# Two tiles of a second block: products of the identity with zeros in front of TensorE's sums and weight waits

## The reference, cut to what matters

```
for l in range(DEPTH):                                   # DEPTH = 2
    ...                                                  # attention, retention, y
    h_res = h_res + y
    hf = rms_norm_2(h_res, ffn_norm_g[l])
    gate, up = jnp.split(hf @ w_gate_up[l], 2, axis=-1)  # 1024 x 5632
    h_res = h_res + (jax.nn.silu(gate) * up) @ w_down[l] # 2816 x 1024
return h_res[:, N_META:]
```

## Time and profile before

| | us |
|---|---|
| median of 3 runs | 2458.93 |
| the profiled execution | 2453.13 |
| its span | 2451.3 |
| TensorE matmul busy | 2145.9 (88%) |
| VectorE busy | 1576.1 (64%) |
| mean granted TensorE clock | 0.947 of full speed |

### The profile page before, as it was taken

How to read it: one execution, slowest core, us unless ns; L and a number is a source line. 1 busy time by engine, 2 the same in 40 slices (tenths; PEclk the granted TensorE clock), 3 DMA queues, 4 the chain that set the end, 5 groups by cost and what they waited for, 6 DMA issues and landing times. The chain is left out here.

```text
span 2451.3 us, 40115 instructions
## 1 busy us (share of the span) xinstructions
PE 2145.9 (88%) x16356; PEld 1987.4 (81%) x16356; DVE 1576.1 (64%) x4195; ACT 462.8 (19%) x1004; POOL 637.4 (26%) x518
## 2 busy tenths in 40 slices
PE   9998899777879868697996788887998899999999
PEld 7887789777769868676896786787868898899799
DVE  1259688786778768768787888888688533212310
ACT  2221232101024111112301133100331012102100
POOL 0024334243334334333333413232233200000000
PEclk9999999988989989899998987999989899999999
DMA  8599999999999999999999998999989969568474
GB/s 324 194 390 422 420 421 419 422 421 413 422 421 418 420 411 420 421 420 407 390 421 420 421 360 315 390 423 421 415 337 419 421 234 386 183 242 315 172 259 154
DMA packets 107205, 901.21 MB, mean 368 GB/s; under 512 B 12780, under 2 KB 16912, under 8 KB 18320
## 3 DMA queue, kind: packets, MB, share of 16 engines
q0 software_dynamic: 73904, 537.43, 53.6%
q1 hardware_dynamic: 31872, 357.95, 36.8%
q10 hardware_dynamic: 1248, 3.28, 0.4%
HBM read 897.57 MB, written 1.05 MB: 367 GB/s over the span
## 5 line engine op out<-in xcount | busy, mean ns | idle before, releaser
L2500 POOL DMA_INDIRECT row<-in_experts,idx x448 | 559.9, 1250 | 1176.3 <-DVE acc L2059 544.3
L2076 DVE CUSTOM_DVE_ANT_0 row<-row,h2n 128x1024 f32<-128x1024 f32 x448 | 534.8, 1221 | 184.9 <-DMA row<-in_experts,idx 183.8
L918 PE MATMUL ea<-diag,row 128*128 128x128 f32 x3808 | 487.8, 292 | 141.3 <-DVE diag L2098 141.3
L918 PEld LDWEIGHTS ea<-diag,row 128*128 128x128 f32 x3808 | 476.1, 208 | 155.2 <-DVE diag L2098 153.6
L2059 DVE SCALAR_TENSOR_TENSOR acc<-row,wgt,acc 128x1024 f32<-128x1024 f32 x207 | 265.2, 1281 | 2.0
L1550 ACT ACTIVATE gl<-dots 128x4 f32<-128x4 f32 x128 | 26.3, 205 | 953.2 <-DVE dots L2076 953.1
L1000 PE MATMUL ea<-hB,wring 128*128 128x144 f32 (+1 forms) x1056 | 144.2, 299 | 15.0 <-DMA wring<-in_weights 15.0
L1000 PEld LDWEIGHTS ea<-hB,wring 128*128 128x128 f32 x1056 | 140.2, 203 | 17.5 <-DMA wring<-in_weights 16.8
L1000 PE MATMUL pa<-hB,wring 128*128 128x144 f32 (+1 forms) x1056 | 132.5, 285 | 13.7 <-DMA wring<-in_weights 11.1
L1000 PEld LDWEIGHTS pa<-hB,wring 128*128 128x128 f32 x1056 | 128.8, 190 | 17.1 <-DMA wring<-in_weights 12.4
L810 PE MATMUL pa<-hA,wring 128*128 128x128 f32 x960 | 123.1, 281 | 0.0
(11 more groups left out here) (553 smaller groups left out, 3255.3 us busy)
## 6 DMA issues: line engine op xcount, KB each, us to landing
wring<-in_weights SPq DMA_DIRECT2D x110, 2048.0 KB, 11.8
wlate<-in_weights SPq DMA_DIRECT2D x25, 2048.0 KB, 7.8
wring<-in_weights SPq DMA_DIRECT2D x22, 1408.0 KB, 6.4
wlate<-in_weights SPq DMA_DIRECT2D x10, 1408.0 KB, 6.2
more<-in_weights SPq DMA_DIRECT2D x5, 2048.0 KB, 7.9
row<-in_experts,idx POOLq DMA_INDIRECT x448, 18.9
row<-in_weights SPq DMA_DIRECT2D x3, 2048.0 KB, 16.8
wring<-in_weights SPq DMA_DIRECT2D x3, 1792.0 KB, 11.3
```

What stands on the lines that cost most here:

```text
L918: m = pe.matmul(EA[c // 4][:, (c % 4) * P:(c % 4 + 1) * P], v[:, c * P:(c + 1) * P], diag[:, DIAG_SLOTS * (q % 2) + i, :], start=False, st ...
L2076: dve.tensor_tensor_reduce(out=r, in0=r, in1=h2n[:, u % 2, :], scale=1.0, scalar=0.0, op0=ALU.mult, op1=ALU.add, accum_out=dots[:, g % 2, ...
L2500: pool.indirect_dma_start(out=expert_rows[slot], out_offset=None, in_=table, in_offset=bass.IndirectOffsetOnAxis(ap=idx[:, k % 3, GB * g + ...
```

## The change

A helper `filler(name, n)` is added. In units of the first tile only (v = 0 and 1) it asks for the bank of the group that comes next and issues n products of the identity with zeros, 512 columns each, into it, with no signal at their end. The group's own first product starts the bank afresh. It stands in three places: 5 products in front of the sums `st2`, 4 in front of each `weights` wait of j = 1 to 10, and 6 in front of each `weights` wait of dn0 to dn7. That is 5 + 40 + 48 = 93 products for each unit, 186 in all. Nothing is taken away.

```diff
+                def filler(name, n):
+
+                    if not t:
+                        b = group(name)
+                        for _ in range(n):
+                            pe.matmul(b[:], ident, zeros, start=True, stop=True)
+
...
                 features("g0", w, (0, P), xr, KC, P, raw)
+                filler("st2", 5)
                 column_sums("st2", both(hB, None), 2)
...
                 for j in range(1, FC // 2):
+                    filler(f"g{j}", 4)
                     w = weights(8 + j, KC)
                     features(f"g{j}", w, (0, P), hB, KC, P, ("b_h", {k: KC + k + 1 for k in range(KC)}) if j == 1 else None)
...
                 for c in range(KC):
+                    filler(f"dn{c}", 6)
                     w = weights(8 + FC // 2 + c, FC, FC * P)
```

## The result

The changed kernel takes 2542.3 us (median of 4, 2539.46 to 2552.83) against 2459.5 us: ratio 1.0348, 95% interval 1.0332 to 1.0364. It is slower, as forecast, but by 83 us (86 us by the ratio) and not by 19; the time lies far outside the range. In the changed profile the span is 2537.6 us, 86.3 us more.

What follows compares the result with a forecast made beforehand. The prediction took memory to bound the kernel up to about 1960 us and TensorE to be busy from 1979 us on. Its terms, 17.2 + 1 + 1 = +19.2 us on the 2458.9 us median, gave 2478 us, range 2466 to 2488.

Steps and rivals of the forecast that it cites:

- One product: Price of one added product on TensorE, read from L911: 0.43 us, so both units' 186 cost 80 us.
- The sign that the prediction named: Unit 1's dn0 starting within a few us of 1979 us; 10 us sooner or later would make the prediction wrong.
- Part 1: Unit 1's down steps: 48 products, 20.7 us, in the open, less 3.5 us of waits filled: +17.2 us.
- Part 2: Unit 1's st2 and gate-and-up steps: 45 products, 19.4 us, mostly in waits, against 20.2 us of room: +1 us.
- The walk through the steps: Unit 1's gate-and-up steps: TensorE some 6.3 us late at the end of j = 5, +1.6 us by j = 10.
- Part 3: Unit 0: 93 products, 40 us, nearly all in waits and time lost at the lower clock: +1 us.
- The sum: All stretches together: 17.2 + 1 + 1 = +19.2 us, a forecast median of 2478 us.
- The waits don't absorb: Rival, 15%: in the two stretches before 1979 us the greatest lateness is kept, +28.2 us, 2487.1 us.
- The whole of the clock is a gain: Rival, 10%: all fillers before 1979 us fall in waits and 11.2 us of low clock come off, +6.0 us.
- Not slower: Rival, 4%: tiles issued sooner also remove the wait and slow start of unit 1's g0, -0.5 us, 2458.4 us.
- it doesn't do what it says: Rival, 2%: the products don't occupy TensorE in the down steps, so nothing moves, 2458.9 us.
- The clock: Before 1979 us, fillers in waits keep TensorE at 2.4 GHz, worth 5.3 us in unit 1 and 5.9 in unit 0.

## Why the prediction was wrong, step by step

**One product: this step failed.** The prediction put "four in a row take 1.89 us" as four products. They are two. L911 stands in a loop over two banks, and its count over the kernel, x12 in the earlier trace rows, is three clearings of two banks, so six products. The text ahead makes the same mistake where it calls a down step 44 products (its loop has 22, and the profile shows 44 instructions) and g_j and u_j 32 each (16 in the source). The pitch of 0.43 us was right for an instruction and half of the price of a product, which is 3.45 / 4 = 0.8625 us; the added work was 160 us and not 80. The forecast's bounds took the price as given, and so did its rivals, except for the one in which the products cost nothing; none reached the result, and the chance for it was nil in my cases. The sign that the prediction named did show: dn0's first filler starts at 2028.6 us, not within a few us of 1979.

**Part 1, unit 1's down steps: mechanism right, the term mis-sized.** With 48 x 0.8625 = 41.4 us less the 3.5 us of waits it gives +37.9. Profile after: 88.9 us in place of 51.8, +37.2. The waits there are gone, unit 2 then takes the same 420 us, and by itself the part costs +41 us (35 to 47). For +17 us of it the forecast needed products of half the price.

**Part 2, unit 1 before the down steps.** 45 x 0.8625 = 38.8 us less the 20.2 us of room is +18.6. Profile after: 131.6 us in place of 116.5, +15.2, which holds 2.5 us of g0 at the higher clock, whose wait was shorter this time. The room of waits and clock was about right. The walk through the steps (6.3 us late, then caught up) did not take place: a gate step took 11.3 us, its tiles landed 10.1 us (median of nine) after they were issued, and no step waited for one. Its sum was also short by 0.6 us: 2.2 + 1.3 + 6.9 - 3.5 is 6.9.

**Part 3, unit 0.** 93 x 0.8625 = 80.2 us less 33.2, 3.7 and 5.9 us is +37.4. Profile after: 221.4 us in place of 186.3, +35.1; by itself +35 us. "VectorE and a full memory set this stretch" holds for the 40 us that the forecast counted (187.0 us with half the columns) and not for 80: there TensorE sets it, and the memory falls to a share of 0.90.

**The sum** with the price put right is 37.9 + 18.6 + 37.4 = +94 us against 86 in the profile. With half the columns the added work is the forecast's, and so is the time: +19 us measured, +19.2 forecast. That the sum agrees is partly luck in its parts: in that profile unit 1's down steps, with dn0's filler, take 68.5 us in place of 51.8, +16.7 (17.2 forecast), unit 1 before them +3.3 and unit 0 +0.7 (1 and 1).

**The rivals.** The kernel with half the columns adds just the 80 us that the rivals reckoned with, and tests them by its +19 us (14 to 25). "The waits don't absorb" (+28.2) lies outside: 61 of 80 us were absorbed, and 74 of 160 in the whole change. "The whole of the clock is a gain" (+6.0) lies outside too, although the granted clock there is 0.99 and 1.00 in the two stretches; the two kernels with filler in the long waits alone gained 4 us, at most 7. "Not slower" and "it doesn't do what it says" were wrong.

**The clock.** As forecast, the lower clock left both stretches: in the changed profile it is 1.00 in unit 1 and 0.99 in unit 0, where the earlier trace rows have 0.92 and 0.95. The Trainium skill, "TensorE: Matmul & The Clock Gate", section "HAM oscillation — how this bites in real kernels", which the prediction named, is borne out on both halves: the slow start, here after some waits and not after all, and the cure by denser work. What the cure costs where it goes beyond the wait, the 83 us show.

## What to carry to other kernels

Before a trace's duration becomes the price of a source line, divide the number of its instructions in the trace by the number of calls in the loops: in float32 each product was two. Work put in front of a wait was free here up to the length of that wait and cost its full length beyond: 30 us ahead of unit 1's down steps were free, 80 us over all the places cost 19 and 160 us cost 83. Filling the longest waits to hold the clock was worth 4 us (1 to 7), and the waits of one profile are not those of every execution.

## What the runs showed of the hardware

A product with a 128x128 identity against 512 columns of zeros took 0.86 us of TensorE in float32 (two instructions of 0.43 us), 0.43 us with 256 columns, 0.22 us with 128, and 0.22 us in bfloat16 with 512 columns. With products of zeros between the kernel's own, TensorE kept its 2.4 GHz: from unit 0's g1 to dn7 of the changed kernel (1569 to 1771 us) the granted clock is 1.00.
